# A weight in four quarters instead of two halves: the start of a two-block transformer kernel on one core

## What is computed

```python
c_act = jax.nn.silu(c)
mod = c_act @ w_ada[l] + b_ada[l]                       # 1024 -> 6 * 1024
sh1, sc1, gt1, sh2, sc2, gt2 = jnp.split(mod, 6, axis=-1)
h = modulate(rmsnorm(x, g_mix[l]), sh1, sc1)            # h * (1 + sc1) + sh1
proj = h @ w_in[l]                                      # q, k, v, pool and conv inputs
v = proj[..., o_k:o_v]                                  # 512 columns
...
x = x + gt1[:, None, :] * mixed
```

## Time and profile before

| | us |
|---|---|
| median of 3 runs | 1746.83 |
| lowest and highest run | 1744.95, 1747.18 |
| profiled execution | 1745.7 |
| its span | 1743.9 |
| PE busy in the span | 1690.7 (97%) |
| DVE, ACT busy | 822.0, 613.9 |

### The profile page before, as it was taken

The page is one execution under the profiler, slowest core; times in us unless marked ns, Lnnn a source line. Parts: engine busy times, 40 slices in busy tenths (PEclk is TensorE's granted clock), DMA queues, the critical chain, the costliest instruction groups (busy, mean ns, idle before and its releaser), DMA issues.

```text
span 1743.9 us, 22780 instructions
## 1 busy us (share of the span) xinstructions
PE 1690.7 (97%) x8075; PEld 1362.3 (78%) x8075; DVE 822.0 (47%) x1273; ACT 613.9 (35%) x1064; POOL 138.8 (8%) x142
## 2 busy tenths in 40 slices
PE   6999899999999999999999999999999999999997
PEld 4766577888888887888888887777788888888886
DVE  4788756443333334444444435666455444444322
ACT  3465534222222323222222222555443422223222
POOL 0002101000001112000000030002001100000000
PEclk9999999999999999999999999999999999999999
DMA  8643113443333325333343336212232333333331
GB/s 333 209 134 112 46 55 103 134 131 98 97 101 97 100 86 152 96 96 96 96 119 100 95 106 135 65 50 69 81 96 88 97 96 96 96 96 108 102 99 65
DMA packets 299791, 184.57 MB, mean 106 GB/s; under 512 B 15179, under 2 KB 286023, under 8 KB 299719
## 3 DMA queue, kind: packets, MB, share of 16 engines
q1 hardware_dynamic: 294112, 169.89, 32.6%
q0 software_dynamic: 3968, 12.70, 3.0%
q10 hardware_dynamic: 1656, 1.25, 0.3%
HBM read 180.67 MB, written 6.36 MB: 107 GB/s over the span
## 4 chain that ended last, share of the span: by engine, by line
PE 88%; DVE 6%; DMA 2%; ACT 2%; issue 2%; SPq 1%; DVEq 0%; ACTq 0%
PE psum L549 28%; PE psum L551 27%; PE psum L550 27%; DVE w_lo L1550 1%; PE psum L962 1%; PE psum L937 1%; PE psum L745 1%; PE psum L980 1%; DMA w_raw<-in_ffn_w_gate 1%; ACT w_hi L1147 1%; DVE p L1689 1%; DVE acc L1543 1%; DMA w_raw<-in_w_in 1%; PE psum L705 1%; DMA sq<-in_w_ada 1%
## 5 line engine op out<-in xcount | busy, mean ns | idle before, releaser
L549 PE MATMUL psum<-h_hi,w_hi 128*128 128x512 f32 x1480 | 588.7, 398 | 14.5 <-DVE w_lo L1550 6.5
L551 PE MATMUL psum<-h_hi,w_lo 128*128 128x512 f32 x1480 | 577.9, 390 | 0.0
L550 PE MATMUL psum<-h_lo,w_hi 128*128 128x512 f32 x1480 | 577.9, 390 | 0.0
L1550 DVE TENSOR_TENSOR w_lo<-w_raw,w_hi 128x1024 fp32r<-128x1024 f32 (+2 forms) x266 | 352.7, 1326 | 326.4 <-ACT w_hi L1147 322.9
L549 PEld LDWEIGHTS psum<-h_hi,w_hi 128*128 128x128 f32 x1480 | 278.3, 188 | 99.1 <-issue 26.7
L1147 ACT ACTIVATE w_hi<-w_raw 128x1024 fp32r<-128x1024 f32 (+2 forms) x266 | 288.1, 1083 | 149.7 <-PE psum L551 134.5
L551 PEld LDWEIGHTS psum<-h_hi,w_lo 128*128 128x128 f32 x1480 | 278.3, 188 | 59.2
L550 PEld LDWEIGHTS psum<-h_lo,w_hi 128*128 128x128 f32 x1480 | 278.6, 188 | 56.0 <-issue 1.0
L549 PE MATMUL psum<-hid_hi,w_hi 128*128 128x512 f32 x528 | 205.8, 390 | 0.0
L551 PE MATMUL psum<-hid_hi,w_lo 128*128 128x512 f32 x528 | 205.7, 390 | 0.0
L550 PE MATMUL psum<-hid_lo,w_hi 128*128 128x512 f32 x528 | 205.7, 390 | 0.0
(11 more groups left out here) (244 smaller groups left out, 1380.4 us busy)
## 6 DMA issues: line engine op xcount, KB each, us to landing
w_raw<-in_w_in SPq DMA_DIRECT2D x50, 512.0 KB, 3.7
w_raw<-in_w_gate_up SPq DMA_DIRECT2D x44, 512.0 KB, 3.6
w_raw<-in_ffn_w_gate SPq DMA_DIRECT2D x44, 512.0 KB, 3.6
w_raw<-in_ffn_w_up SPq DMA_DIRECT2D x44, 512.0 KB, 3.7
w_raw<-in_ffn_w_down SPq DMA_DIRECT2D x32, 704.0 KB, 4.3
sq<-in_w_ada SPq DMA_DIRECT2D x24, 512.0 KB, 4.5
w_raw<-in_w_down SPq DMA_DIRECT2D x16, 704.0 KB, 4.4
ada_w<-in_w_ada SPq DMA_DIRECT2D x16, 512.0 KB, 10.8
```

Source lines behind the costliest of these rows:

```text
L549: pe.matmul(o, a_hi, b_hi, start=start, stop=False)
L550: pe.matmul(o, a_hi, b_lo, start=False, stop=False)
L551: return pe.matmul(o, a_lo, b_hi, start=False, stop=stop)
L1550: dve.tensor_tensor(w_lo[:, s % 2, 0:n], w_raw[:, s % 2, 0:n], w_hi[:, s % 2, 0:n].bitcast(F32), ALU.subtract).then_inc(w_ready, 1)
```

## The change

- `w_ada`'s first 2048 columns come in four quarters (`ada_part`, `PARTS` = 4): 8 transfers each, of 256 KB, with 256 columns of shift and 256 of scale. SP's order becomes quarter 0, slab 0, quarter 1, slab 1, quarter 2, slab 2, quarter 3, slab 3. Each quarter modulates the two channel tiles that the slab behind it multiplies.
- On PE `first_rows(s + 1)` stands before token tile 1 of slab s and `first_columns(s + 1)` before tile 2, for s = 0 to 2. A product of `first_rows` is 128 columns wide instead of 256.
- On DVE and ACT the loop runs over four parts of two tiles: row copy, sums, two `hm`, the slab's `w_lo`, two `h_lo`; ACT splits slab h ahead of its two `h_hi`.
- The vectors are split: the first three (`FIRST_ROWS`, bias, c and g_mix) are turned ahead of x, the other nine after `first_columns(0)` ("late_vectors"). 20 transposes of the identity (`warm`) stand ahead of the first, 8 after the second. ACT makes the activated vector before the sums of squares.
- Rows 2 to 5 of the first gate get homes of their own in `wt`, with a semaphore each. Rows 0 and 1 are loaded after slab 3; rows 2 to 5 after slab 4 once `h_ready` is 7; rows 6 and 7 after slab 5. `split_low(4)` to `(6)` stand each before two `mod_step`.
- The transfers of the lambdas and the sink, `dist`, the counts and `turn_m` move from ACT to POOL, and `rpb_rows` from POOL's beginning to behind them.

```diff
         def row_slab(r):
-            return min(step_slab(r - 2) + 2, S_SIDE - 1) if r >= 2 else 1
+            if r < KD:
+                return 3 if r < 2 else 4 if r < 6 else 5
+            return min(step_slab(r - 2) + 2, S_SIDE - 1)
+
+        def row_home(r):
+
+            return wt_rows[:, D * (r - 2):D * (r - 1)] if 2 <= r < 6 else ada_row[:, r % 2, :]
...
             pe.wait_ge(const_landed, 16)
+            warm(20, 7, 3 * P)
+            pe.wait_ge(rows_landed, 16 * 3)
+            pe.transpose(psum[:, 7, 0:FIRST_ROWS], rows[0:FIRST_ROWS, :], ident[0:FIRST_ROWS, 0:FIRST_ROWS])\
+              .then_inc(filled[7], 1)
             pe.wait_ge(x_landed, 16 * TT)
...
-                        at = D * (g // 2) + T * h + 2 * P * (g % 2)
-                        last = pe.matmul(psum[DQ1 * g:DQ1 * g + DQ1, b, 0:2 * P], cact_wide[:, k, :],
-                                         ada_w[:, k, at:at + 2 * P], start=k == 0, stop=k == KD - 1)
+                        at = D * (g // 2) + KP * P * h + RW * (g % 2)
+                        last = pe.matmul(psum[DQ1 * g:DQ1 * g + DQ1, b, 0:RW], cact_wide[:, k, :],
+                                         ada_w[:, k, at:at + RW], start=k == 0, stop=k == KD - 1)
...
-            first_rows(0, range(0, 2))
+            first_rows(0, range(8))
             pe.wait_ge(x_normed, 1)
...
-            first_rows(0, range(2, KD))
             first_columns(0)
+            pe.wait_ge(late_rows_landed, 16 * (len(VECTORS) - 3))
+            b = take("late_vectors")
+            pe.transpose(psum[:, b, FIRST_ROWS:N_ROWS], rows[FIRST_ROWS:N_ROWS, :], ident[FIRST_ROWS:N_ROWS, FIRST_ROWS:N_ROWS])\
+              .then_inc(filled[b], 1)
+            warm(8, 7, 3 * P)
...
                 for i in range(TT):
-                    if s == S_V + 1 and i == 1:
-                        first_rows(1, range(6, KD))
-                    if s == S_V + 1 and i == 2:
-                        first_columns(1)
+                    if s < S_V + 3 and i == 1:
+                        first_rows(s + 1, range(KD))
+                    if s < S_V + 3 and i == 2:
+                        first_columns(s + 1)
...
-                if s == S_V:
-                    first_rows(1, range(6))
...
-            ada_half(0)
+            ada_part(0)
...
-                        if r >= 2:
-                            sp.wait_ge(mod_added, r - 1)
+                        if r == 2:
+                            sp.wait_ge(h_ready, KP * (PARTS - 1) + 1)
+                        elif r >= 6:
+                            sp.wait_ge(mod_added, r - 5 if r < KD else r - 1)
                         mod_row(sp, r)
 
             for s in range(4):
+                if s:
+                    ada_part(s)
                 free(s)
                 load(s, w1[:, 2 * s:2 * s + 2, o_v:o_v + T], n=T)
-                if s == 1:
-                    ada_half(1)
                 mod_rows_after(s)
...
-            for h in range(2):
-                for k in range(4 * h, 4 * h + 4):
+            for h in range(PARTS):
+                split_high(h)
+                for k in range(KP * h, KP * h + KP):
...
-            for h in range(2):
+            for h in range(PARTS):
+                copy_rows(h)
+                first_mods(h)
                 dve.wait_ge(mod_set, h + 1)
                 b = wait_filled(dve, "x_scale")
-                for k in range(4 * h, 4 * h + 5):
-                    if k < 4 * h + 4:
+                for k in range(KP * h, KP * h + KP + 1):
+                    if k < KP * h + KP:
...
+                    if k == KP * h + 1:
+                        split_low(h)
...
+            mod_step(1)
+            for s in range(4, 7):
+                split_low(s)
+                for r in range(2 * s - 6, 2 * s - 4):
                     mod_step(r)
...
-            pool.dma_start(rpb_rows, ins["rpb"].unsqueeze(0).to_broadcast([COLS + 1, n_rpb])).then_inc(rpb_copied, 16)
-
+            pool.wait_ge(h_ready, 2)
...
             pool.wait_ge(h_ready, KD)
+            pool.dma_start(dist[:, :], ins["k_dist"]).then_inc(dist_landed, 16)
```

More of the change, by code:

```diff
@@ L32 @@
 KF = FF // P
+PARTS = 4
+KP = KD // PARTS
+RW = T // PARTS
 HALF = KF // 2
@@ L296, in program @@
         rows_landed, x_landed, const_landed = sem("rows_landed"), sem("x_landed"), sem("const_landed")
+        turn_landed = sem("turn_landed")
+        wide_landed = [sem(f"wide_landed{n}") for n in range(4)]
         lam_landed, dist_landed, table_landed = sem("lam_landed"), sem("dist_landed"), sem("table_landed")
@@ L570, in _, with warm @@
             hs = [(h_hi[:, k, :], h_lo[:, k, :]) for k in range(KD)]
+            def warm(n, b=3, at=0):
+                for _ in range(n):
+                    pe.transpose(psum[:, b, at:at + P], ident[:, :], ident[:, :])
             pe.wait_ge(const_landed, 16)
+            warm(20, 7, 3 * P)
+            pe.wait_ge(rows_landed, 16 * 3)
+            pe.transpose(psum[:, 7, 0:FIRST_ROWS], rows[0:FIRST_ROWS, :], ident[0:FIRST_ROWS, 0:FIRST_ROWS])\
+              .then_inc(filled[7], 1)
             pe.wait_ge(x_landed, 16 * TT)
@@ L597, in first_columns @@
                 b = take(("mod0", h))
-                for n in range(2):
-                    last = pe.matmul(psum[:, b, n:KD:2], mod_rows[:, 2 * P * h + P * n:2 * P * h + P * n + P],
+                for n in range(RW // P):
+                    at = RW * h + P * n
+                    last = pe.matmul(psum[:, b, n:2 * KP:RW // P], mod_rows[:, at:at + P],
                                      ident[:, 0:P:DQ1], start=True, stop=True)
                 last.then_inc(filled[b], 1)
-            turned(x_tok, "x", range(0, 4))
-            pe.wait_ge(rows_landed, 16 * len(VECTORS))
-            pe.transpose(psum[:, 7, 0:N_ROWS], rows[0:N_ROWS, :], ident[0:N_ROWS, 0:N_ROWS]).then_inc(filled[7], 1)
-            turned(x_tok, "x", range(4, KD))
+            turned(x_tok, "x")
             pe.wait_ge(cact_set, 2)
-            first_rows(0, range(0, 2))
+            first_rows(0, range(8))
             pe.wait_ge(x_normed, 1)
@@ L783, in out_proj @@
                     two(2, i)
-            def warm(n, b=3):
-                for _ in range(n):
-                    pe.transpose(psum[:, b, 0:P], ident[:, :], ident[:, :])
             def token_sums(name, phase, kinds=1):
@@ L1147, in split_high @@
                 act.activation(w_hi[:, s % 2, 0:n], w_raw[:, s % 2, 0:n], ACT.Identity).then_inc(w_high, 1)
+            act.wait_ge(consts_set, N_CONSTS)
+            wait_emptied(act, "vectors")
+            c0 = ROW_OF["c"]
+            act.activation(cact[:, :], vcol[:, c0:c0 + KD], ACT.Silu).then_inc(cact_set, 1)
+            act.activation(cact_wide[:, :, 0:1], vcol[:, c0:c0 + KD].unsqueeze(2), ACT.Silu).then_inc(cact_set, 1)
             act.wait_ge(x_landed, 16 * TT)
-            act.wait_ge(consts_set, N_CONSTS)
             for i in range(TT):
@@ L1157, in _ @@
             act.activation(rcol[:, 4:8], rcol[:, 0:4], ACT.Sqrt, bias=eps, scale=1.0 / D).then_inc(x_root, 1)
-            wait_emptied(act, "vectors")
-            c0 = ROW_OF["c"]
-            act.activation(cact[:, :], vcol[:, c0:c0 + KD], ACT.Silu).then_inc(cact_set, 1)
-            act.activation(cact_wide[:, :, 0:1], vcol[:, c0:c0 + KD].unsqueeze(2), ACT.Silu).then_inc(cact_set, 1)
-            split_high(0)
-            for h in range(2):
-                for k in range(4 * h, 4 * h + 4):
+            for h in range(PARTS):
+                split_high(h)
+                for k in range(KP * h, KP * h + KP):
                     act.wait_ge(x_normed, k + 2)
```

116 lines of the change are left out of this document (55 added, 61 removed).

## The result

| | before | after |
|---|---|---|
| median of 16 runs, us | 1747.16 | 1750.17 |
| lowest and highest, us | 1744.95, 1748.76 | 1748.15, 1753.74 |
| profiled execution, its span, us | 1745.7, 1743.9 | 1748.15, 1746.4 |
| first product of slab 0 | 27.59 | 23.64 |
| slab 3 starts | 54.22 | 52.77 |

The ratio is 1.002, 95% interval 1.0013 to 1.0027: **slower by 0.2%**, 3.0 us, where no change was forecast.

What follows compares the result with a forecast made beforehand. TensorE, busy 97% of the span, was taken to bound the kernel, so only the mixing start counts: -4.7 + 1.1 + 0.7 + 2.9 = 0.0 us, median 1746.8; range 1741.5 to 1752.5 (8 in 10).

Steps and rivals of the forecast that it cites:

- the forecast's sign: Whole kernel: same time, within the 3.5 us a measurement can tell; chance 0.44.
- Part 1: Start up to slab 0's first product: 22.9 instead of 27.59 us, -4.7.
- Part 2: Value slabs, slab 0 to slab 3: 27.7 instead of 26.6 us, +1.1, with PE standing 1.5 us at each of three slabs.
- R: Time of a quarter's 64 modulation row products on PE: taken as 1.95 us, between 1.8 and 3.65.
- the second rival: Slabs 0 to 2: modulation rows cost per instruction, R stays 3.65; price 5.1 us, time 1751.9; chance 0.12.
- the last one: Modulation row products: weight loads do not overlap, R = 5.8; +11.6 us, 1758.4; chance 0.03.
- The clock at the start: PE idle before slab 0: a clock fall costs +1.5 us, no fall 0; half taken, +0.7.
- Part 3: Slab 3 to the mixing stage: late slab 5, slab 6 and gate rows end the columns at +22.3 against 19.4, +2.9.
- The faster one: Rival: tail free (+0.6), clock stays up (0), R 1.7; -3.7 us, 1743.1; chance 0.27.
- the third: Rival: burst behind h_ready 7 at 299 GB/s (+2.6), table load before the squares (+1.3); 1750.7; chance 0.09.
- One to one behind 73.65: From the mixing start at 73.65 us on: a shift of that start shifts the end equally.

Runs made afterwards that it cites:

- silu_preload: Changed kernel with a dummy Silu activation ahead of ScalarE's wait for the vectors, to load the table earlier; 1749.58 us, ratio 1.0015.
- low_ahead: Changed kernel with w_lo of slabs 1 to 3 moved ahead of the row copy on VectorE, slab 0's behind the first copy; 1747.02 us, ratio 1.0003.
- second and third profiles: Two further profiled executions of the unchanged changed kernel; 1750.18 and 1752.31 us.
- all_five: Changed kernel with early gate-row release, early Silu load, w_lo ahead of row copies, GpSimd loads behind sixth slab, last gate steps before slab 6's split; 1738.64 us.
- warm_more: Changed kernel with 30 instead of 8 warming transposes ahead of slab 0; 1749.37 us, ratio 1.0021.
- first profile: The first profiled execution of the changed kernel, with nothing altered; 1748.15 us.
- gate_swap: Changed kernel with the last two gate steps ahead of the split of slab 6 on VectorE; 1747.11 us, ratio 0.9998.
- warm_gap: Changed kernel with 30 warming transposes in the gap ahead of slab 5; 1751.56 us, ratio 1.0026.
- slab5_first: Changed kernel with slab 5 issued ahead of the gate's rows 2 to 5; 1752.35 us, ratio 1.0026.
- old_homes: Changed kernel with gate rows 2 to 7 back in the two old homes, two behind each of slabs 4 to 6; 1755.3 us, ratio 1.0042.

## Why the prediction was wrong, step by step

The forecast was no change (1746.8, range 1741.5 to 1752.5); the kernel is 3.0 us slower. The time lies in the range, the forecast's sign does not hold. In the profiled execution the sum forecast for the mixing start was 0.0; measured was +3.3: -3.95 at the start, +2.5 from slab 0 to slab 3, +4.7 in the tail. The two falls of the clock in it, 1.55 us at the start and 1.6 in the tail, are together nearly as large as the miss, and the sum charged them 0.7.

- **Part 1, forecast -4.7, measured -3.95.** The identity, the transposes, the missing load between activated vector and squares, and the columns held. The failed step is "the third load ... now happens while ScalarE (ACT) is idle before x lands". The load stands behind the wait of the instruction that needs it, and that wait ended at 10.25. silu_preload priced it at 1.4 us.
- **Part 2, rows per quarter: right.** R was taken as 1.95 between bounds of 1.8 and 3.65, and is 1.95, which rules out the second rival and the last one. Spacing 9.19 for a forecast 9.25; stall 1.1 for 1.5. The order on DVE that makes the stall was read rightly, and low_ahead removes most of it. A group of six was taken as 1.37 us; the 5.58 us over four from which it comes are 1.40, which adds 0.15 to Part 2 and makes two slabs 11.15 instead of 10.9 (measured 11.15).
- **The clock at the start, forecast +0.7 as a half chance.** From slab 0 to slab 1 it took 10.76 us, and 9.21 in silu_preload, where the clock stayed up. The fall costs 1.55 us, as priced, so 0.85 more than the half that was charged; the spacing gave back 0.15, and the sum from slab 0 to slab 3 is +2.5 for a forecast +1.8. In the second and third profiles the clock was down before slab 0, from 19.9 and 18.8 us on, behind waits of 2.79 and 2.62 us ahead of `x_scale`, which the prediction didn't weigh; slab 0 to slab 1 then took 10.53 and 11.77. Of the sixteen profiles of the changed kernel and its edits only silu_preload and all_five keep the full clock to slab 1, and in warm_more it is back ahead of slab 0. The half chance was too low.
- **Part 3, forecast +2.9, measured +4.7: the step that failed.** The pieces of it were near: slab 5 at +10 (measured +10.65, +10.69, and +12.75 in the first profile), slab 6 at +15.5 (measured +16.65, +17.3), a gap of 1.4 (1.88 and 1.91, or 3.96), steps ending at +20.4 (measured +21.6, +22.2) with "some 2 us" of wait ahead of the columns (2.90). The landings are late in part because GpSimd's transfers were taken as 0.7 MB before slab 6; 1.3 MB are issued by 61.1. What was left out is that the waits have a price beyond themselves. The forecast charged such a price at slab 0, by the earlier trace rows; in Part 3, with a gap of 1.4 us ahead of slab 5 and some 2 ahead of the columns, it charged none and gave no reason. It is 1.6 us inside slab 5 in the first profile (7.19 from slab 5 to the columns, against 5.58), and 1.4 in the columns and 1.8 in the first mixing row in the second. By the second profile, which has the median's time: the start -3.9, slab 0 to slab 3 +2.3, the tail +5.4 (the forecast 2.9, 1.2 of later transfers and 1.4 of clock, rounded), the first mixing row +1.8, together +5.6 at the next mixing row, of which +4.5 is left in the profiled time. The profile of before is 1.5 us below its median, and that leaves the 3.0 us of the medians.
- **The order on DVE.** The prediction named that rows 6 and 7 stand behind slab 6 on DVE and that the columns wait for them. It did not say that this order, reversed against before, was worth 3 us; gate_swap did, with the slab's landing left as it is.
- **The rivals.** The faster one (a free tail and a clock that stays up) had both conditions the wrong way round. Of the third, "the burst behind h_ready 7 goes at 299 GB/s, and a table load stands before the squares", 1750.7, the time fits but half the mechanism doesn't: from 60 to 68 us the engines moved 378 to 397 GB/s, and the load is ahead of the activated vector rather than between it and the squares. Near its time, then, by luck of the sum: for a late slab, a clock and a load in another place.
- **One to one behind 73.65.** The mixing start moved 3.3 and the profiled time 2.45; in the second profile the next mixing row moved 5.6 and the time 4.5. The end follows, to about 1 us.

The clock has one page to be weighed again. The Trainium skill (TensorE: Matmul & The Clock Gate, Part 4: PE-mode transpose) says that transposes don't engage the full clock. No run here agrees: in warm_more PE did nothing but transposes from 19.6 us to 24.2, and the granted clock went from 0.50 (20 to 21 us) to 1.00 (22 to 23); the six products of slab 0 behind them took 1.57 us, where behind the 8 of the second profile of after, with the clock still at 0.50, they took 2.83.

## What to carry to other kernels

When transfers are gathered into a burst with one release, ask which of them the critical engine wants first, when the **last** one lands, and what stands behind it in every queue: here a split that nobody yet needed held the steps that everybody waited for. Give a forecast gap of TensorE a second price, the half clock behind it, wherever in the sum it stands: here it was 1.3 to 2.6 us at slab 0 and 1.6 at slab 5 (behind gaps of 2.5 to 4.3 us), and it also came behind gaps of under 1 us where light work, the one-column products, followed. When two chains end within a few tenths in a profile, look at a second and third execution before naming the bound, and cut both before judging either. And before a profile's gain is called lost, read the granted clock of the whole execution.

## What the runs showed of the hardware

- A transfer of 512 KB took 11.05 us from issue to landing behind 2 MB of its own queue with up to 1.3 MB of GpSimd's beside it, against a median of 3.7 over the kernel, and this landing moved by 2.1 us between executions of the same program.
- Packets of 1 KB cost little: at 25 to 28 us, with quarter 3's transfers (1 KB) and slab 2's (2 KB) under way, the engines moved 394 GB/s, near the 408 of the larger ones.
- 64 products of 32-column weights and 128 columns in four column groups issue in 1.95 us, 0.03 us each at full clock.
- The activation table was loaded behind the wait of the instruction that wants it (at 10.25 us, with ACT idle until then), and ACT's squares after Silu (11.75) needed no load.
- The gate's sixteen one-column products took 1.84 to 1.92 us with the clock up. Behind gaps of 1.5 to 6.2 us they mostly took 2.2 to 3.6 us (1.92 in warm_gap and warm_more, where the clock fell only behind them), and the eight mixing products 2.09 instead of 1.14 (slab5_first, old_homes, low_ahead).
- Falls of the granted clock from 1.00 to 0.50 sit at other places in different executions of one program: in three of after at 24.4, 19.9 and 18.8 us, and at 68.8, 74.5 and 76.8.
